# Feed-forward gate and up projections in two matmuls instead of three: the high weights times the high and low stream as one 512-wide matmul, the halves added at eviction

## The chip, the cores and the metric

The kernel runs on one core of one Trainium2 chip. The metric is the device time of one execution in microseconds, lower is better. The kernel before took 2021.01 us as the median of three runs (2017.32 to 2023.0).

## The reference, cut to what matters

Two transformer-like stacks of two layers each work on a stream of 256 tokens by 1024 channels in float32. Six feed-forward layers lie in them, and the change touches these alone. The first two (conv0, conv1) have a depthwise convolution of width 3 along the tokens between the up projection and the gate; the other four (ffn1.0, ffn2.0, ffn1.1, ffn2.1) have none.

```python
D_MODEL = 1024; SEQ = 256; D_FF = 2816
# conv0, conv1
up = depthwise_conv(h @ ffn_w_up[l], ffn_conv_w[l], ffn_conv_b[l])
f = (jax.nn.silu(up[..., :D_FF]) * up[..., D_FF:]) @ ffn_w_down[l]
h = layer_norm(DEEPNORM_ALPHA * h + f, ln_ffn_g[l], ln_ffn_b[l])
# ffn1.0, ffn2.0, ffn1.1, ffn2.1
gate, up = jnp.split(h @ wi, 2, axis=-1)      # h = rms_norm_2(x, gain)
x = x + 0.5 * ((jax.nn.silu(gate) * up) @ wo)
```

## The kernel before, in words

**Numbers.** Every float32 operand of a projection is split in two float32r parts, high and low, and a product is three matmuls in one PSUM sum: high weights times high stream, high times low, low times high (PASSES). ScalarE writes the high part of the weights as a copy with rounding (w_hi, L1302), VectorE subtracts it from the raw weights (w_lo, L1792). The stream of tokens, transposed so that channels lie on partitions, is split in the same way in xt_hi and xt_lo.

**Units.** Weights come in units of 1 MB (128 partitions x 2048 values) through a ring of three slots: SyncE loads a unit in raw, ScalarE makes w_hi, VectorE makes w_lo and counts unit_split, and TensorE uses it. A unit may be overwritten in w_hi once TensorE has begun the unit after the one that lay in its slot (unit_passed), which is two units before the new one's turn.

**Feed-forward.** The 2816 hidden channels are done in 11 chunks of 256. A chunk needs three units: gate, up, and down. TensorE's order is gate0, up0, then for each chunk c from 1 to 10 gate c, up c, down c-1, and at the end down10; chunks 1 to 10 stand in a hardware loop of five turns. A gate or up unit (up_pair, both_tiles, feature_major) is 2 tiles of 128 channels x 8 blocks k of the contraction x 3 passes = 48 matmuls of 256 columns, all in one bank of 512 values. Gate uses banks 0 and 1 in turn, up 2 and 3. A down unit is 24 matmuls of 512 columns that add to banks 4 to 7. The first gate unit is streamed: it begins when the first blocks of xt are written, k by k.

**What the other engines do with a chunk.** In the four plain layers VectorE multiplies gate's bank by the row factors rb, ScalarE takes the silu, VectorE multiplies silu with up's bank and splits the product in act_hi and act_lo (split_operand), which down needs. In the two layers with a convolution ScalarE writes the center tap of gate and of up (center, L1477), VectorE adds the two side taps of each straight from the bank (taps, four instructions of 255 columns each for gate and for up, L1789), ScalarE takes the silu, and VectorE multiplies and splits. Both engines run strictly in the order written, with the three splits of weight units of the chunk (split_in_loop) in between. On VectorE the third split stands behind split_operand.

The order of work on each engine is written out by hand; semaphores join the engines. The functions touched are both_tiles' caller up_pair and its loop in ffn_any on TensorE, chunk, center and ffn/convffn on ScalarE, gate, chunk, taps on VectorE, and one wait on GpSimd.

## Time and profile before

| | |
|---|---|
| median of three runs | 2021.01 us (2017.32 to 2023.0) |
| the profiled execution | 2020.03 us, its span 2017.5 us |
| TensorE matmul busy | 1909.7 us, 95% of the span |
| VectorE / ScalarE / GpSimd busy | 1277.4 / 893.4 / 103.2 us |
| mean granted TensorE clock | 0.949 |

The profile page gives the busy time of each engine, the busy share in 40 slices, the chain of work that ended last (who released whom, followed back from the end) and the costliest groups of instructions. Matmuls overlap in the record: one takes 283 ns from its start to its end, while the next starts after 120 ns. So durations of matmuls say little here, and starts are what is read. In the order of time a line shows its start in microseconds, its length, the engine, the source line, what is written and read, and how often it follows itself; idle time before it and what ended it stand in brackets.

### The profile page before, as it was taken

Reading aid. Unit: us, or ns where it says so; the run is one execution under the profiler, and the core shown is the slowest. Engines: PE = TensorE matmul, PEld = TensorE weight load, DVE = VectorE, ACT = ScalarE, POOL = GpSimd, SP = SyncE. Lnnn points to the kernel's source line nnn. Section 1 sums busy time; section 2 is a strip of 40 time slices with the busy share of each in tenths; the row PEclk is TensorE's granted clock in tenths of the full one; section 3 lists DMA queues with packets and bytes.
Section 4 is the critical chain, followed back from the end, with each engine's and each line's share of the span. In section 5 each row is a group of like instructions: output and inputs, shape, how many; then the busy total and the mean of one; then the engine's idle time right before and its main releaser. Section 6 shows DMA issues by size and latency. Waiting matters only on the chain.

```text
span 2017.5 us, 31210 instructions
## 1 busy us (share of the span) xinstructions
PE 1909.7 (95%) x12460; PEld 1712.2 (85%) x12460; DVE 1277.4 (63%) x1585; ACT 893.4 (44%) x1076; POOL 103.2 (5%) x79
## 2 busy tenths in 40 slices
PE   7989999988899999999988999999999989999999
PEld 7966899985699989998976888999999875789998
DVE  5787777688687776556545646556555657546555
ACT  5444444544454444335442445333533444445332
POOL 0300200030020000000060000000000000000000
PEclk9988899998899989999985999999999995999999
DMA  8531455552155545554522445555555430235553
GB/s 298 188 129 43 156 184 184 185 165 78 63 189 186 187 146 191 187 187 147 182 70 84 151 156 174 184 182 182 167 183 185 145 134 13 85 124 168 187 187 125
DMA packets 226931, 310.79 MB, mean 154 GB/s; under 512 B 6630, under 2 KB 199430, under 8 KB 226214
## 3 DMA queue, kind: packets, MB, share of 16 engines
q1 hardware_dynamic: 224038, 298.07, 44.2%
q0 software_dynamic: 2528, 10.14, 1.6%
q10 hardware_dynamic: 288, 1.52, 0.2%
q8 instruction: 53, 0.87, 0.2%
q14 instruction: 24, 0.20, 0.0%
HBM read 306.56 MB, written 3.15 MB: 154 GB/s over the span
## 4 chain that ended last, share of the span: by engine, by line
PE 85%; DVE 8%; ACT 3%; issue 2%; POOL 1%; DMA 1%; DVEq 0%; ACTq 0%
PE bank L660 43%; PE bank L887 17%; PE bank L787 8%; PE bank L683 4%; PE bank L669 3%; PE bank L960 2%; PE bank L932 2%; DVE work L1789 2%; PE bank L716 1%; ACT w_hi L1302 1%; DVE w_lo L1792 1%; PE bank L946 1%; DVE work L1792 1%; PE bank L1204 1%; DVE work L2451 1%
## 5 line engine op out<-in xcount | busy, mean ns | idle before, releaser
L1792 DVE TENSOR_TENSOR w_lo<-raw,w_hi 128x2048 fp32r<-128x2048 f32 x280 | 640.1, 2294 | 391.1 <-ACT w_hi L1302 390.7
L1302 ACT ACTIVATE w_hi<-raw 128x2048 fp32r<-128x2048 f32 x280 | 533.0, 1904 | 742.8 <-PE bank L660 467.7
L660 PE MATMUL bank<-xt_hi,w_hi 128*128 128x256 f32 x2560 | 728.4, 285 | 1.0 <-DVE w_lo L1792 1.0
L660 PE MATMUL bank<-xt_lo,w_hi 128*128 128x256 f32 x2560 | 725.5, 283 | 0.0
L660 PE MATMUL bank<-xt_hi,w_lo 128*128 128x256 f32 x2560 | 725.3, 283 | 0.0
L660 PEld LDWEIGHTS bank<-xt_hi,w_hi 128*128 128x128 f32 x2560 | 492.0, 192 | 6.5 <-issue 2.4
L660 PEld LDWEIGHTS bank<-xt_lo,w_hi 128*128 128x128 f32 x2560 | 491.9, 192 | 3.0 <-issue 0.7
L660 PEld LDWEIGHTS bank<-xt_hi,w_lo 128*128 128x128 f32 x2560 | 491.8, 192 | 0.0
L887 PE MATMUL bank<-w_hi,act_hi 128*128 128x512 f32 x528 | 206.5, 391 | 0.0
L887 PE MATMUL bank<-w_lo,act_hi 128*128 128x512 f32 x528 | 206.2, 390 | 0.0
L887 PE MATMUL bank<-w_hi,act_lo 128*128 128x512 f32 x528 | 205.4, 389 | 0.0
L887 PEld LDWEIGHTS bank<-w_hi,act_lo 128*128 128x128 f32 x528 | 99.2, 188 | 21.1
L887 PEld LDWEIGHTS bank<-w_hi,act_hi 128*128 128x128 f32 x528 | 99.4, 188 | 19.9 <-DVE act_lo L1792 0.9
L887 PEld LDWEIGHTS bank<-w_lo,act_hi 128*128 128x128 f32 x528 | 99.4, 188 | 18.2
L1789 DVE SCALAR_TENSOR_TENSOR work<-bank,par,work 128x255 f32<-128x255 f32 (+2 forms) x212 | 92.3, 478 | 23.7 <-ACT work L1477 17.3
L787 PE MATMUL bank<-w_hi,act_hi 128*128 128x512 f32 x224 | 89.9, 401 | 6.7 <-ACT work L1611 3.0
L1302 ACT ACTIVATE work<-bank 128x512 f32<-128x512 f32 (+6 forms) x88 | 46.8, 541 | 102.9 <-PE bank L946 46.5
L787 PE MATMUL bank<-w_lo,act_hi 128*128 128x512 f32 x224 | 88.9, 397 | 0.0
L787 PE MATMUL bank<-w_hi,act_lo 128*128 128x512 f32 x224 | 88.7, 396 | 0.0
L932 PE MATMUL bank<-work 128*128 128x256 f32 (+3 forms) x192 | 63.7, 505 | 18.2 <-DVE work L1792 9.1
L683 PE MATMUL bank<-xt_hi,w_hi 128*128 128x256 f32 x192 | 59.3, 309 | 18.4 <-DVE xt_lo L1789 10.7
L1477 ACT ACTIVATE work<-bank,par 128x256 f32<-128x256 f32 x88 | 44.5, 556 | 64.6 <-PE bank L660 64.6
(287 smaller groups left out, 2134.2 us busy)
## 6 DMA issues: line engine op xcount, KB each, us to landing
raw<-in_ffn_wi SPq DMA_DIRECT2D x88, 1024.0 KB, 5.1
raw<-in_ffn_w_up SPq DMA_DIRECT2D x44, 1024.0 KB, 5.1
raw<-in_ffn_wo SPq DMA_DIRECT2D x44, 1024.0 KB, 4.8
raw<-in_ffn_w_down SPq DMA_DIRECT2D x22, 1024.0 KB, 5.4
raw<-in_w_in SPq DMA_DIRECT2D x14, 1024.0 KB, 5.4
raw<-in_ssd_in_proj SPq DMA_DIRECT2D x14, 1024.0 KB, 5.3
raw<-in_mem_wkv SPq DMA_DIRECT2D x9, 1024.0 KB, 7.0
raw<-in_w_out SPq DMA_DIRECT2D x8, 1024.0 KB, 5.1
```

What stands on the lines that cost most here:

```text
L660: ins = first(mm(dst, w[s][:, k, c0:c0 + m], xt[v][:, k, :], start=k == 0 and p == 0, stop=k == KT - 1 and p == 2))
L669: ins = first(mm(dst, xt[s][:, k, P * tt:P * tt + P], w[v][:, k, c0:c0 + n], start=start and k == 0 and p == 0, stop=k == KT - 1 and p == 2))
L683: ins = first(mm(dst[:, T * j:T * j + T], w[s][:, k, P * j:P * j + P], xt[v][:, k, :], start=k == 0 and j == 0 and p == 0, stop=k == KT - ...
L716: ins = pe.transpose(bank[b][:, T * half + P * tt:T * half + P * tt + P], src[:, tt, P * k:P * k + P], ident)
L787: ins = first(mm(bank[b][:, :], act[s][:, u % 2, r, P * tt:P * tt + P], w[v][:, r, HALF * h:HALF * h + HALF], start=u == 0 and r == 0 and ...
L887: ins = first(mm(bank[b][:, :], act[s][:, c % 2, j, P * tt:P * tt + P], w[v][:, j, HALF * h:HALF * h + HALF], start=False, stop=True, skip ...
L932: ins = mm(bank[b][:, at:at + n], d["q"][t][c], d["k"][c][:, 0:n], start=c == 0, stop=c == len(d["k"]) - 1)
L960: ins = mm(bank[b][r:r + m, T * c + q0:T * c + T], v[s], prob_t[:, h % 2, T * s:T * s + T - q0], start=s == 0, stop=s == TT - 1 or d["keys ...
L1302: return act.activation(dst, src, ACT.Copy)
L1477: ins = act.activation(dst[:, c % 2, j, :], bank[b][:, T * j:T * j + T], ACT.Identity, scale=par[:, cw, at], bias=par[:, cb, at])
L1789: return dve.scalar_tensor_tensor(out=out, in0=in0, scalar=scalar, in1=in1, op0=op0, op1=op1)
L1792: return dve.tensor_tensor(out=out, in0=in0, in1=in1, op=op)
```

## The change

A gate or up unit is now 2 tiles x 8 blocks x 2 matmuls (wide_tiles). The first reads xt_hi and xt_lo of one block k as one moving operand of 512 columns (they are now two halves of one tensor, xt_both) and writes a whole bank: high times high in its columns 0 to 255, high times low in 256 to 511. The second is low weights times high stream, 256 columns, added to columns 0 to 255. A tile of 128 channels now takes a bank of its own, so gate takes banks 0 and 1 for every chunk and up 2 and 3, with no second pair to alternate with: TensorE waits for pair_drained of the last chunk before it begins the next. ScalarE copies the low halves of the two banks to f_low (low_half), and VectorE adds them to the other halves (whole); its result goes to f_gate, f_up or, in the layers with a convolution, to f_sum, from which center and taps now read. In the plain layers the multiplication of gate by rb is an instruction of its own behind the addition. In the layers with a convolution VectorE's order changes as well. The broadcast of the row factors goes through bank 4 instead of bank 1.

```diff
@@ -294,15 +302,17 @@
-        bank = [ctx.enter_context(nc.psum_tensor(f"bank{b}", [P, HALF], F32)) for b in range(8)]
+        psum = ctx.enter_context(nc.psum_tensor("bank", [P, 8, HALF], F32))
+        bank = [psum[:, b, :] for b in range(8)]
-        xt_hi = sb("xt_hi", [P, KT, T], F32R)
-        xt_lo = sb("xt_lo", [P, KT, T], F32R)
+        xt_both = sb("xt", [P, 2, KT, T], F32R)
+        xt_hi = xt_both[:, 0, :, :]
+        xt_lo = xt_both[:, 1, :, :]
...
@@ -685,6 +702,27 @@
+            def wide_tiles(b, w, first, done):
+
+                def tile(k, j):
+                    dst, part = bank[b + j], slice(P * j, P * j + P)
+                    first(mm(dst[:, :], w[0][:, k, part], xt_both[:, :, k, :], start=k == 0, stop=False,
+                             skip_group_check=True))
+                    ins = mm(dst[:, 0:T], w[1][:, k, part], xt_hi[:, k, :], start=False, stop=k == KT - 1,
+                             skip_group_check=True)
+                    if k == KT - 1 and j == 1:
+                        ins.then_inc(done, 1)
+
+                if stream_due:
+                    for k in range(KT):
+                        stream_tile(k)
+                        for j in range(2):
+                            tile(k, j)
+                else:
+                    for j in range(2):
+                        for k in range(KT):
+                            tile(k, j)
+
@@ -850,23 +888,20 @@
                     pe.wait_ge(unit_split, q0 + k + 1 if turns is None else turns * 6 + q0 + k + 1)
                     return [w[:, (q0 + k) % RING, :].rearrange("p (a b) -> p a b", a=a) for w in (w_hi, w_lo)]
-                def up_pair(k, b, turns):
-
-                    w = split_unit(k, turns, KT)
-                    both_tiles(bank[b], w, First()).then_inc(bank_full[b], 1)
-
-
-                claim(0, f"{tag}.g0")
-                up_pair(0, 0, None)
-                claim(2, f"{tag}.u0")
-                up_pair(1, 2, None)
+                def up_pair(k, i, turns):
+                    wide_tiles(2 * i, split_unit(k, turns, KT), First(), pair_full[i])
+
+                for i in range(2):
+                    for b in (2 * i, 2 * i + 1):
+                        pe.wait_ge(bank_drained[b], names.fills[b])
+                    up_pair(i, i, None)
                 if scaled:
                     pe.wait_ge(row_ready, seen.next(row_ready))
-                    claim(1, f"{tag}.rb")
+                    claim(4, f"{tag}.rb")
                     for tt in range(TT):
-                        ins = mm(bank[1][:, P * tt:P * tt + P], rcol[:, tt:tt + 1].broadcast_to([P, P]), ident,
+                        ins = mm(bank[4][:, P * tt:P * tt + P], rcol[:, tt:tt + 1].broadcast_to([P, P]), ident,
                                  start=True, stop=True)
-                    ins.then_inc(bank_full[1], 1)
+                    ins.then_inc(bank_full[4], 1)
                 for tt in range(TT):
                     for h in range(2):
                         claim(4 + 2 * tt + h, f"{tag}.{tt}{h}")
@@ -896,18 +931,15 @@
                         for tt, h in ORDER:
                             rows_of(tt, h)
-                base = {b: names.fills[b] for b in range(4)}
-                with pe.Fori(0, TURNS, 1) as i:
+                with pe.Fori(0, TURNS, 1) as turn:
                     for c in (1, 2):
                         k = 2 + 3 * (c - 1)
-                        for b, kk in ((c % 2, k), (2 + c % 2, k + 1)):
-                            pe.wait_ge(bank_drained[b], base[b] + i)
-                            up_pair(kk, b, i)
-                        down(k + 2, c - 1, i)
-                for c in (1, 2):
-                    for b, what in ((c % 2, "g"), (2 + c % 2, "u")):
-                        names.of[f"{tag}.{what}{c}"] = (b, base[b] + 1)
-                        names.fills[b] = base[b] + TURNS
+                        for i in range(2):
+                            pe.wait_ge(pair_drained[i], turn * 2 + chunk_count(tag, c - 1))
+                            up_pair(k + i, i, turn)
+                        down(k + 2, c - 1, turn)
+                for i in range(2):
+                    pe.wait_ge(pair_drained[i], chunk_count(tag, NCHUNK - 1))
                 down(len(unit_names) - 1, NCHUNK - 1, None, last=True)
                 seen.next(act_split, NCHUNK)
...
+            def low_half(tag, what, c, turn):
+                i = "gu".index(what)
+                act.wait_ge(pair_full[i], chunk_count(tag, c) if turn is None else turn * 2 + chunk_count(tag, c))
+                copy(f_low[:, 2 * i:2 * i + 2, :], psum[:, 2 * i:2 * i + 2, T:2 * T]).then_inc(low_ready, 1)
             def ffn(kind, l):
                 tag = f"{kind}.{l}"
-                def chunk(c, name, turn):
-                    b, n = names.of[name]
-                    act.wait_ge(bank_drained[b], n if turn is None else turn + n)
+                def chunk(c, turn):
+                    low_half(tag, "g", c, turn)
+                    act.wait_ge(gate_ready, seen.next(gate_ready))
                     act.activation(f_silu[:, c % 2, :], f_gate[:, c % 2, :, :], ACT.Silu).then_inc(silu_ready, 1)
+                    low_half(tag, "u", c, turn)
...
+                def center(c, what, dst, tile0, turn):
+                    low_half(tag, what, c, turn)
+                    i = "gu".index(what)
+                    act.wait_ge(pair_drained[i], chunk_count(tag, c) if turn is None else turn * 2 + chunk_count(tag, c))
+                    for j in range(2):
+                        t = tile0 + 2 * c + j
+                        at = bass.ds(44 + t, 1) if turn is None else bass.ds(turn * 4 + 44 + t, 1)
+                        ins = act.activation(dst[:, c % 2, j, :], f_sum[:, 2 * i + j, :], ACT.Identity,
+                                             scale=par[:, cw, at], bias=par[:, cb, at])
+                    ins.then_inc(center_ready, 1)
+                def chunk(c, turn):
+                    center(c, "g", f_gate, 0, turn)
+                    center(c, "u", f_up, 22, turn)
+                    if turn is not None:
+                        split_in_loop(tag, 3 * c + 3, turn)
+                    act.wait_ge(taps_ready, seen.next(taps_ready))
+                    act.activation(f_silu[:, c % 2, :], f_gate[:, c % 2, :, :], ACT.Silu).then_inc(silu_ready, 1)
...
@@ -2040,24 +2081,27 @@
                 if split_next[0] < len(split_order):
                     split_late.append(True)
+            def whole(tag, what, c, turn, dst):
+                i = "gu".index(what)
+                dve.wait_ge(low_ready, seen.next(low_ready))
+                dve.wait_ge(pair_full[i], chunk_count(tag, c) if turn is None else turn * 2 + chunk_count(tag, c))
+                tt_(dst, psum[:, 2 * i:2 * i + 2, 0:T], f_low[:, 2 * i:2 * i + 2, :],
+                    ALU.add).then_inc(pair_drained[i], 1)
+                dve.wait_ge(pair_drained[i], chunk_count(tag, c) if turn is None else turn * 2 + chunk_count(tag, c))
             def ffn(kind, l):
                 tag = f"{kind}.{l}"
                 def gate(c, turn):
-                    b, n = names.of[f"{tag}.g{c}"]
-                    dve.wait_ge(bank_full[b], n if turn is None else turn + n)
-                    tt_(f_gate[:, c % 2, :, :], two(bank[b][:, :]), spread(rb[:, :], 2),
-                        ALU.mult).then_inc(bank_drained[b], 1)
+                    whole(tag, "g", c, turn, f_gate[:, c % 2, :, :])
+                    tt_(f_gate[:, c % 2, :, :], f_gate[:, c % 2, :, :], spread(rb[:, :], 2),
+                        ALU.mult).then_inc(gate_ready, 1)
                 def chunk(c, turn):
+                    whole(tag, "u", c, turn, f_up[:, c % 2, :, :])
                     dve.wait_ge(silu_ready, seen.next(silu_ready))
-                    b, n = names.of[f"{tag}.u{c}"]
-                    dve.wait_ge(bank_full[b], n if turn is None else turn + n)
-                    tt_(f_raw[:, c % 2, :], f_silu[:, c % 2, :], bank[b][:, :],
-                        ALU.mult).then_inc(bank_drained[b], 1)
-                    dve.wait_ge(bank_drained[b], n if turn is None else turn + n)
+                    step(tt_(two(f_raw[:, c % 2, :]), two(f_silu[:, c % 2, :]), f_up[:, c % 2, :, :], ALU.mult))
                     split_operand(c % 2, two(f_raw[:, c % 2, :]))
                 split()
...
+                def total(c, what, turn):
+                    i = "gu".index(what)
+                    whole(tag, what, c, turn, f_sum[:, 2 * i:2 * i + 2, :])
+                def taps(c, what, dst, tile0, turn):
                     dve.wait_ge(center_ready, seen.next(center_ready))
-                    b, n = names.of[name]
+                    i = "gu".index(what)
                     for g, side in ((wa, 0), (wb, 1)):
                         for j in range(2):
                             t = tile0 + 2 * c + j
                             w = par[:, g, bass.ds(t, 1) if turn is None else bass.ds(turn * 4 + t, 1)]
                             part = dst[:, c % 2, j, 1:T] if side == 0 else dst[:, c % 2, j, 0:T - 1]
-                            src = bank[b][:, T * j:T * j + T - 1] if side == 0 else bank[b][:, T * j + 1:T * j + T]
+                            src = f_sum[:, 2 * i + j, 0:T - 1] if side == 0 else f_sum[:, 2 * i + j, 1:T]
                             ins = stt(part, src, w, part, ALU.mult, ALU.add)
                         if side == 0:
                             step(ins)
-                    ins.then_inc(bank_drained[b], 1)
+                    return ins
                 def chunk(c, turn):
-                    taps(c, f"{tag}.g{c}", f_gate, 0, turn)
-                    taps(c, f"{tag}.u{c}", f_up, 22, turn)
-                    b, n = names.of[f"{tag}.u{c}"]
-                    dve.wait_ge(bank_drained[b], n if turn is None else turn + n)
+                    total(c, "g", turn)
+                    if turn is not None:
+                        split_in_loop(tag, 3 * c + 2, turn)
+                    taps(c, "g", f_gate, 0, turn).then_inc(taps_ready, 1)
+                    total(c, "u", turn)
+                    if turn is not None:
+                        split_in_loop(tag, 3 * c + 3, turn)
+                    step(taps(c, "u", f_up, 22, turn))
                     dve.wait_ge(silu_ready, seen.next(silu_ready))
                     step(tt_(two(f_raw[:, c % 2, :]), two(f_silu[:, c % 2, :]), f_up[:, c % 2, :, :], ALU.mult))
                     split_operand(c % 2, two(f_raw[:, c % 2, :]))
-                    if turn is not None:
-                        split_in_loop(tag, 3 * c + 3, turn)
```

Where the instructions now stand is shown at two places. The first is VectorE in the loop of the two layers with a convolution, the second (up) half of a chunk. Before, from the wait for the center tap to the splits of the next units:

```order
L1789 ISA [waits center_ready]
L1789 SCALAR_TENSOR_TENSOR work<-bank,par,work 128x255
...
L1789 ISA [waits vec_step]
L1789 SCALAR_TENSOR_TENSOR work<-bank,par,work 128x255
...
L1792 TENSOR_TENSOR work<-work 128x512 [waits silu_ready]
L1827 CAST act_hi<-work 128x512 [waits vec_step]
L1792 TENSOR_TENSOR act_lo<-work,act_hi 128x512 [waits vec_step]
L1792 TENSOR_TENSOR w_lo<-raw,w_hi 128x2048 [waits hi_ready]
```

Now the same place, in which low_ready is ScalarE's copy of the low halves, pair_full_u TensorE's end of the up unit, and hi_ready ScalarE's split of the unit after next:

```order
L1833 TENSOR_TENSOR work<-bank,work 128x512 [waits pair_full_u,low_ready]
L1862 REGISTER_ALU [waits pair_drained_u]
L1833 TENSOR_TENSOR w_lo<-raw,w_hi 128x2048 [waits hi_ready]
L1830 ISA [waits center_ready]
L1830 SCALAR_TENSOR_TENSOR work<-work,par 128x255
...
L1830 ISA [waits vec_step]
L1830 SCALAR_TENSOR_TENSOR work<-work,par 128x255
...
L1833 TENSOR_TENSOR work<-work 128x512 [waits silu_ready,vec_step]
L1868 CAST act_hi<-work 128x512 [waits vec_step]
L1833 TENSOR_TENSOR act_lo<-work,act_hi 128x512 [waits vec_step]
```

The addition is new, and the split of the third unit moved from behind the last subtraction to ahead of the up taps.

The second place is TensorE at the start of a plain layer, from the end of up0 to the first matmul of gate1. Before:

```order
L867 MATMUL bank1<-con,rcol 128x128 [waits bank_drained1,row_ready]
L867 MATMUL bank1<-con,rcol 128x128
L874 MATMUL bank4<-zero 128x512 [waits bank_drained4]
L874 MATMUL bank5<-zero 128x512 [waits bank_drained5]
...
L850 ISA [waits bank_drained1]
L660 MATMUL bank1<-xt_hi,w_hi 128x256 [waits unit_split]
```

Now:

```order
L902 MATMUL bank<-con,rcol 128x128 [waits bank_drained4,row_ready]
L902 MATMUL bank<-con,rcol 128x128
L909 MATMUL bank<-zero 128x512 [waits bank_drained4]
L909 MATMUL bank<-zero 128x512 [waits bank_drained5]
...
L888 ISA [waits pair_drained_g]
L709 MATMUL bank<-xt,w_hi 128x512 [waits unit_split]
L711 MATMUL bank<-xt,w_lo 128x256
```

The four zeroing matmuls now stand behind the drain of the row factors' bank, and gate1 behind VectorE's addition of gate0 instead of behind that drain alone.

## Rows read from the trace of the kernel before

**Rows 1.** The page, parts 1 and 4.

```profile
PE 1909.7 (95%) x12460; PEld 1712.2 (85%) x12460; DVE 1277.4 (63%) x1585; ACT 893.4 (44%) x1076; POOL 103.2 (5%) x79
PE bank L660 43%; PE bank L887 17%; PE bank L787 8%; PE bank L683 4%; PE bank L669 3%; PE bank L960 2%; PE bank L932 2%; DVE work L1789 2%; PE bank L716 1%; ACT w_hi L1302 1%; DVE w_lo L1792 1%; PE bank L946 1%; DVE work L1792 1%; PE bank L1204 1%; DVE work L2451 1%
```

**Rows 2.** Chain in order of time in conv0: start us, length us, what.

```profile
297.92 11.51 PE bank L660 x96
...
394.33 5.47 PE bank L887 x24
399.81 3.03 PE bank L887 x12
```

**Rows 3.** TensorE in order of time: 27 matmuls in a row, then 14.

```profile
624.74 0.28 PE L660 MATMUL bank<-xt_hi,w_hi 128*128 128x256 f32 x1
...
627.86 0.28 PE L660 MATMUL bank<-xt_hi,w_lo 128*128 128x256 f32 x1
...
1282.64 0.39 PE L887 MATMUL bank<-w_lo,act_hi 128*128 128x512 f32 x1
...
1285.59 0.39 PE L887 MATMUL bank<-w_hi,act_lo 128*128 128x512 f32 x1
```

**Rows 4.** VectorE in order of time, one chunk of conv0.

```profile
305.78 2.29 DVE L1792 TENSOR_TENSOR w_lo<-raw,w_hi 128x2048 fp32r<-128x2048 f32 x1 [3.46 <-ACT w_hi L1302]
307.99 1.89 DVE L1789 SCALAR_TENSOR_TENSOR work<-bank,par,work 128x255 f32<-128x255 f32 x4
...
312.98 0.69 DVE L1792 TENSOR_TENSOR work<-work 128x512 f32<-128x512 f32 x1 [0.32 <-ACT work L1489]
313.71 0.43 DVE L1827 CAST act_hi<-work 128x512 fp32r<-128x512 f32 x1
...
314.77 4.52 DVE L1792 TENSOR_TENSOR w_lo<-raw,w_hi 128x2048 fp32r<-128x2048 f32 x2
```

**Rows 5.** ScalarE in order of time, the same chunk.

```profile
309.61 1.02 ACT L1477 ACTIVATE work<-bank,par 128x256 f32<-128x256 f32 x2 [2.95 <-PE bank L660]
310.52 1.91 ACT L1302 ACTIVATE w_hi<-raw 128x2048 fp32r<-128x2048 f32 x1
```

**Rows 6.** Groups by line and shape: count, busy us, mean ns, idle before.

```profile
L1789 DVE SCALAR_TENSOR_TENSOR work<-work,par 128x256 f32<-128x256 f32 x134 | 56.6, 479 | 0.8 <-DVE work L1789 0.4
L1792 DVE TENSOR_TENSOR work<-work,bank 128x512 f32<-128x512 f32 x46 | 31.7, 689 | 63.0 <-PE bank L660 56.8 <-ACT work L1452 4.5 <-PE bank L1093 1.8
L1302 ACT ACTIVATE work<-bank 128x512 f32<-128x512 f32 x51 | 29.9, 592 | 57.2 <-PE bank L946 29.2 <-POOL mix L2604 16.8 <-PE bank L660 6.7
```

**Rows 7.** Start of ffn1.1: ScalarE's drain of rb; the chain on TensorE.

```profile
1425.92 0.38 ACT L1302 ACTIVATE rb<-bank 128x256 f32<-128x256 f32 x1 [4.10 <-PE bank L867]
...
1425.89 0.96 PE bank L874 x4
1426.85 11.71 PE bank L660 x96
```

**Rows 8.** Start of ffn1.0: VectorE's splits; the chain.

```profile
764.83 4.49 DVE L1792 TENSOR_TENSOR w_lo<-raw,w_hi 128x2048 fp32r<-128x2048 f32 x2 [1.50 <-ACT w_hi L1302]
...
767.18 11.77 PE bank L660 x96
```

**Rows 9.** VectorE ahead of gate0 of ffn1.1.

```profile
1412.11 2.68 DVE L1789 SCALAR_TENSOR_TENSOR xt_lo<-bank,par,xt_hi 128x256 fp32r<-128x256 f32 x6 [0.58 <-ACT xt_hi L1335]
```

**Rows 10.** TensorE after idle time; a stretch, with granted clock behind POOL's busy time.

```profile
408.86 1.94 PE L716 MATMUL bank<-con,mix 128*128 128x128 f32 x16 [3.31 <-DVE mix L1979]
...
746.34 3.65 PE L716 MATMUL bank<-con,mix 128*128 128x128 f32 x16 [3.31 <-DVE mix L1979]
...
751.30:755.20 3.90, 3.89 (x18) 3.90 (x19) 3.80 (x7) 1.41 (x4) 0.00 (x0) 0.50 0.00 0
```

**Rows 11.** VectorE and GpSimd near the start of conv0.

```profile
232.86 2.53 DVE L1827 CAST act_hi<-work 128x512 fp32r<-128x512 f32 x1
...
232.35 2.75 POOL L2524 TENSOR_TENSOR x<-x,wide 128x1024 f32<-128x1024 f32 x1
```

More of the change, by code:

```diff
@@ L202, in weight_units, with chunk_count @@
     return place
+FFN_ORDER = ("conv0", "conv1", "ffn1.0", "ffn2.0", "ffn1.1", "ffn2.1")
+def chunk_count(tag, c):
+    return NCHUNK * FFN_ORDER.index(tag) + c + 1
 class Count:
@@ L2615, in swa @@
             def swa():
-                full("ffn1.1.g0")
+                pool.wait_ge(pair_full[0], chunk_count("ffn1.1", 0))
                 pool.dma_start(w_bias[0:1, 0:D], inp["attn_bo_2"][0:1, :]).then_inc(small_in, 16)
```

32 lines of the change are left out of this document (17 added, 15 removed).

## The prediction

> **What bounds the kernel now.** I read the page first [rows 1]: TensorE's matmuls fill 95% of the span, and in the chain that ended last the gate and up line L660 alone holds 43%, the down line L887 17%. The reader is to see that VectorE, at 63%, isn't the bound on average. Then the chain in order of time [rows 2]: inside a feed-forward layer it holds nothing but TensorE, 96 matmuls of a gate and an up unit in 11.51 us and 24 of a down unit in 5.47 us, so a chunk takes 16.98 us, and what is saved on TensorE is saved for good as long as nobody else is late. Third, TensorE's starts [rows 3]: 26 steps of 256 columns take 3.12 us, or 0.1200 us each; 13 steps of 512 columns take 2.95 us, or 0.2269 us each. Two narrow ones cost 0.2400, one wide one 0.2269. The columns are the same, so a matmul with its weight load has a fixed part of about 13 ns.
>
> **The gain.** There are 6 layers x 11 chunks x 2 units x 2 tiles x 8 blocks = 2112 places where two narrow matmuls become one wide. 2112 x 0.0131 = 27.7 us. At the half clock there is no fixed part to save: 18 matmuls of 256 columns in 3.90 us are 0.217 each [rows 10], which is 256 columns at 1.2 GHz. The cold start of gate0 in ffn1.0, and the same taken for conv0, take 0.3 off: 27.4 us. A chunk should take 16.98 - 32 x 0.0131 = 16.56 us.
>
> The row says 13 ns. The Trainium skill (TensorE: Matmul & The Clock Gate, "Wait — 56ns, not 53.3ns?") has start-to-start of a warm matmul at N / 2.4 GHz plus about 2.5 ns. By that the gain would be 2112 x 2.5 ns = 5.3 us, an estimate from that page. The trace disagrees with it and decides; the sum doesn't use it.
>
> No matmul before reads its moving operand in two runs. I bound its extra cost by 0 from below (the down matmul reads 512 in one run at 0.2269) and by 13 ns from above, at which a wide one costs as much as two narrow ones. I take 0, since the column rate is the same in both rows of starts. The Trainium skill (SBUF — State Buffer, "Door 1: The DMA port swizzle (why `[64,N]` ≈ `[32,N]`)", the note on cachelines) says that accesses that stay on a 16-byte line run at full bandwidth; the two runs here are 1 KB each, so by it too nothing is lost. No run before shows it.
>
> **What is added.** Per chunk ScalarE gets two copies of 128x512 out of PSUM, near 0.59 us each, and VectorE two additions of 128x512 with one operand in PSUM, near 0.69 us each [rows 6]. In the plain layers gate's addition is new beside the multiplication, and so is up's. The side taps now read both operands from SBUF: 479 ns there [rows 6] against four in 1.89 us with one from PSUM [rows 4], no difference. In the plain layers VectorE has three splits at 2.29 and some 4 us of small work in 16.56 us; the copies and additions hide behind up and down.
>
> **Layers with a convolution, in the loop.** VectorE's round per chunk, from starts [rows 4, 5]: three splits x 2.22 (305.78 to 307.99) = 6.7; taps 2 x 1.9 = 3.8; product, cast and subtraction 312.98 to 314.77, 1.8; additions 2 x 0.72 = 1.4. Then a wait that is new: the third split now stands between up's addition and up's taps, ScalarE splits its part behind the center tap, and the center tap waits for that addition. ScalarE's center pair to its split is 0.91 (309.61 to 310.52), the split 1.91, with hand-overs 2.9 in all. Sum 16.6, beside TensorE's 16.56. So the two engines are level. I take no stall per chunk in the loop, with a bound of 0.6 us per chunk above (below). Without that wait in the order VectorE had 13.7 us of work and the cover would be ample.
>
> **Layers with a convolution, at the end.** Down10 follows down9 without another gate and up between. It needs act_lo of chunk 10, and before that came just in time: down9 starts at 394.33 and takes 5.47, and down10 starts at 399.81, with no idle time [rows 2]. Now, from the end of gate10 (t): ScalarE first splits the unit after (to t+2.0, released by the start of up10), copies the low half (t+2.6), VectorE adds (3.3), splits (5.5), taps (7.4), adds up (8.1), ScalarE does center and split (11.0), VectorE splits (13.2), taps (15.1), product, cast, subtraction and hand-over (17.1). TensorE is ready at t + 5.55 (up10) + 5.47 (down9) = 11.0. Stall 6.0 us, twice: 12.1. TensorE idle for 3.31 us was followed by transposes at half speed, 16 in 3.65 us [rows 10], and by matmuls at granted clock 0.50, 1.2 GHz, in the 3.9 us from 751.30. After 6 us of idle I expect the same: some 3.4 us of down10 at half rate, 1.7 us lost, twice: 3.4. Bounds 0 and 2 each.
>
> **Plain layers, at the start.** ffn2.0, ffn1.1, ffn2.1: before, gate1 starts at 1426.85 behind the zeroing matmuls, which ran from 1425.89 beside the drain of rb (1425.92 to 1426.30) [rows 7]. Now the zeroing waits for that drain (0.45 later), and gate1 waits for ScalarE's copy (0.59) and VectorE's addition (0.69) behind the drain, so it starts near 1427.7: 0.9 later, three times: 2.7. In ffn1.0 VectorE is late at this point: its two splits run from 764.83 to 769.3, and gate1 starts at 767.18, behind the first [rows 8]. The addition of gate0 stands behind both, so gate1 starts at 770.1: 2.9 later, and 0.3 of gain in gate0 and up0 is lost with it. I add 0.5 for a chance that the clock falls in that gap: 3.7.
>
> **Streamed gate0.** It now waits for banks 0 and 1, that is for block 3 of xt instead of block 2. In the plain layers with a stream from PSUM blocks come every 0.45 us (six in 2.68) [rows 9], and TensorE needs 0.7 per block, so it can't catch up: 3 x 0.45 = 1.3. In conv0, conv1 and ffn1.0 ScalarE has drained both banks by then: 0.
>
> **Sum.** Against the profiled execution, 2020.03 us (span 2017.5 and 2.5 around it): -27.4 + 12.1 + 3.4 + 2.7 + 3.7 + 1.3 = -4.2 us. Beside them GpSimd: near 232 us its additions of 2.75 us go along with a cast of 2.53 us on VectorE that takes 0.43 elsewhere [rows 11, 4]. VectorE's round in conv0 and conv1 now has more reads from SBUF and no slack at its start; 0.5 each: -3.2. The profiled execution is 1.0 below the median of the runs; from one or the other I get 2016.8 to 2017.8. I say 2017.
>
> **The rivals.**
> A. VectorE's side costs less: the clock doesn't fall in the gaps, and the end stall is nearer 5 us since hand-overs overlap. For it: the transposes at 408.86, also after 3.31 us of idle, took 1.94 us for 16, near full speed [rows 10]. Against: 6 us of idle is almost twice 3.31. Sum: -3.2 - 3.4 - 2 = -8.6: 2011.
> B. Slower: the loops of conv0 and conv1 become bound by VectorE. The round is 16.6 by durations; six more waits per chunk on VectorE at 0.1 us each make 17.2, and from 16.56 on each tenth counts in 20 rounds: 0.6 x 20 = 12, so 2029. For it: no slack is left, and a new ring ScalarE to VectorE to ScalarE to VectorE lies in each round. Against: the waits that exist cost 0.03 us, as between product and cast (312.98 + 0.69 to 313.71) [rows 4].
> C. The change doesn't do what it says: the wide matmul costs as much as two narrow ones, by its two-run operand or since the fixed part belongs to bytes and not to instructions. The gain vanishes and the costs stay: 2044. Against: the starts [rows 3]. By the page's 2.5 ns (TensorE: Matmul & The Clock Gate, in the Trainium skill) it would come out near here too, at 2039, an estimate.
>
> **How the numbers follow.** Forecast (gain and costs nearly cancel, 2013 to 2021) 0.55, A (2008 to 2013) 0.22, B (2023 to 2032) 0.16, C 0.04, others 0.03. What a measurement of this kernel can tell from no change is about 0.3%, 6 us: below 2015.0 is faster, above 2027.1 slower. Faster takes all of A and a fourth of the forecast: 0.35. Slower is most of B and C: 0.15. Same is the rest, 0.50. The range leaves out C and the tails of A and B: 2008 to 2027.
>
> **What the profile after would show.** Right: starts of a wide and a narrow one 0.347 us apart; 16.56 us per chunk in ffn loops; TensorE waiting for VectorE's act_lo at the end of conv0 and conv1 for 6 us, with the clock at 0.5 behind it; gate1 waiting in the plain layers 0.9 us, in ffn1.0 some 4 us in all. Wrong: a pair above 0.36 us (C), chunks of conv0 above 16.7 us with TensorE waiting for w_lo or act_lo in the loop (B), or no wait at the ends (A).

## The result and the profile after

The changed kernel takes 2048.42 us (median of 4 runs, 2044.95 to 2053.49), the kernel before on the same chip 2019.16 (4 runs). The ratio is 1.014, with a 95% interval of 1.0119 to 1.0161. It is slower by 29 us where I forecast some 3 less; the time lies outside my range (2008 to 2027), and "slower" had 0.15. A kernel's time is always the median over its executions in the fast state; the only other one, of 10147.63 us in experiment 8, is left out.

The page of the changed kernel, parts 1 and 4, against [rows 1]:

```profile
PE 1910.4 (93%) x10348; PEld 1607.5 (79%) x10348; DVE 1360.9 (67%) x1717; ACT 966.3 (47%) x1208; POOL 102.7 (5%) x79
PE 80%; DVE 10%; ACT 4%; issue 4%; POOL 1%; DMA 1%; DVEq 0%; ACTq 0%
```

TensorE has 2112 instructions less and is as long busy: what the pairs save is made up by stretches at half clock, in which a matmul is longer (down10, gate1 of ffn1.0 and others below), so the busy time hides the gain. VectorE and ScalarE now hold 14% of the chain that ended last. Starts of the same work in both chains show where:

| from there | before, us | after, us | after minus before |
|---|---|---|---|
| output rows of mixer 0 | 185.00 | 184.73 | -0.3 |
| down10 of conv0 | 399.81 | 408.86 | +9.1 |
| output rows of mixer 1 | 524.72 | 535.51 | +10.8 |
| down10 of conv1 | 737.30 | 760.43 | +23.1 |
| last downs of ffn1.0 | 931.77 | 959.64 | +27.9 |
| output rows ahead of ffn2.0 | 1196.23 | 1226.78 | +30.6 |
| last downs of ffn1.1 | 1591.38 | 1621.73 | +30.4 |
| last downs of ffn2.1 | 2003.34 | 2031.67 | +28.3 |

The two convolution layers and ffn1.0 lose nearly all of it. Of the other plain layers ffn2.0 loses 0.5 us, ffn1.1 and ffn2.1 gain 0.7 and 1.2. Of the step of 2.7 between ffn1.0 and the rows ahead of ffn2.0, 1.5 us are taken up below.

**The loop.** Down units of ffn2.1 in the chain (start, length):

```profile
1981.29 5.50 PE bank L922 x24
1998.08 5.50 PE bank L922 x24
2014.87 5.50 PE bank L922 x24
```

A chunk takes 16.79 us, not 16.56 ([rows 2]: 16.98 before). Its pairs, and those of up0 in the same layer (a start to the next start of L709 is a pair):

```profile
1887.62 0.40 PE L709 MATMUL bank<-xt,w_hi 128*128 128x512 f32 x1
...
1889.04 0.40 PE L709 MATMUL bank<-xt,w_hi 128*128 128x512 f32 x1
```

```profile
1861.93 0.39 PE L709 MATMUL bank<-xt,w_hi 128*128 128x512 f32 x1
...
1862.96 0.40 PE L709 MATMUL bank<-xt,w_hi 128*128 128x512 f32 x1
```

Four pairs in 1.42, three in 1.03. Over a whole unit it is 5.30 us for 15 pairs in the loops (0.3533 each), and 5.20 in up0 (0.3467, the value that I forecast from [rows 3]). The 0.3533 lies between that and the 0.36 that I had set as the sign of rival C.

**The end of conv0.** VectorE, then ScalarE, then TensorE in order of time:

```profile
391.78 2.29 DVE L1833 TENSOR_TENSOR w_lo<-raw,w_hi 128x2048 fp32r<-128x2048 f32 x1
393.98 0.68 DVE L1833 TENSOR_TENSOR work<-bank,work 128x512 f32<-128x512 f32 x1
394.79 2.29 DVE L1833 TENSOR_TENSOR w_lo<-raw,w_hi 128x2048 fp32r<-128x2048 f32 x1
...
398.82 0.68 DVE L1833 TENSOR_TENSOR work<-bank,work 128x512 f32<-128x512 f32 x1
402.59 2.29 DVE L1833 TENSOR_TENSOR w_lo<-raw,w_hi 128x2048 fp32r<-128x2048 f32 x1 [3.09 <-ACT w_hi L1334]
```

```profile
399.67 1.09 ACT L1518 ACTIVATE work<-work,par 128x256 f32<-128x256 f32 x2 [3.25 <-DVE work L1833]
400.67 1.89 ACT L1334 ACTIVATE w_hi<-raw 128x2048 fp32r<-128x2048 f32 x1
```

```profile
408.86 0.77 PE L922 MATMUL bank<-w_hi,act_hi 128*128 128x512 f32 x1 [8.73 <-DVE act_lo L1833]
409.43 0.63 PE L922 MATMUL bank<-w_lo,act_hi 128*128 128x512 f32 x1
...
412.84 0.63 PE L922 MATMUL bank<-w_hi,act_hi 128*128 128x512 f32 x1
```

The ring that I named is there: up's addition (398.82), ScalarE's center tap and split, VectorE's split 3.09 us later. TensorE waits 8.73 us here and 9.0 in conv1. Then matmuls stand 0.43 apart instead of 0.2267, which is 512 columns at 1.2 GHz (512 / 1.2 GHz = 0.427 us), until about 413.3; in the stretch from 408.90 to 413.00 the granted clock is 0.50, 1.2 GHz. Down10's first twelve take 5.23 us against 3.03 [rows 2].

**The start of conv0.** VectorE's taps for the first gate, with GpSimd beside them:

```profile
229.10 6.14 DVE L1830 SCALAR_TENSOR_TENSOR work<-work,par 128x255 f32<-128x255 f32 x4 [1.24 <-ACT work L1518]
```

```profile
229.57 2.46 POOL L2573 TENSOR_TENSOR x<-mix,wide 128x1024 f32<-128x1024 f32 x1
232.11 2.45 POOL L2574 TENSOR_TENSOR x<-x,wide 128x1024 f32<-128x1024 f32 x1
```

Four taps take 6.14 us, and end after GpSimd has. In the loop they take 1.90. Down0 starts 1.9 us later behind gate0's start than before in conv0, 3.9 in conv1; some 1.6 of the 3.9 are one unit (from 586.67) that runs in part at half clock, 7.10 us from its first to its last start instead of 5.53.

**The start of ffn1.0.** Who TensorE waited for from 776 to 977 us (total, times, longest):

```profile
PE bank L909 <- ACT rb L1334: 3.0, 1, 3.0
PE bank L709 <- DVE work L1833: 2.0, 1, 2.0
PE bank L902 <- DVE rcol L2074: 0.5, 1, 0.5
```

5.5 us where one wait of 1.0 stood before [rows 8], and gate1 behind it runs cold: 15 pairs in 7.33 us instead of 5.30. What ends last is not the wait for rb but VectorE, its two splits and then the addition of gate0:

```profile
789.81 4.49 DVE L1833 TENSOR_TENSOR w_lo<-raw,w_hi 128x2048 fp32r<-128x2048 f32 x2 [1.50 <-ACT w_hi L1334]
794.22 0.68 DVE L1833 TENSOR_TENSOR work<-bank,work 128x512 f32<-128x512 f32 x1
```

```profile
795.03 0.79 PE L709 MATMUL bank<-xt,w_hi 128*128 128x512 f32 x1 [2.00 <-DVE work L1833]
```

VectorE's two splits start 24.98 us later than before (764.83 in [rows 8]), just as gate0 does, and gate1 starts 27.85 later (767.18 there): the start of the layer costs 2.9 us. The waits grew by more, 4.5, because TensorE came to them earlier: gate0 takes 5.63 us at full clock, and took 7.59 before (751.31 to 758.90), when it began at half clock ([rows 10], the stretch from 751.30).

In ffn2.0, ffn1.1 and ffn2.1 the waits for rb and for gate0's sum are 0.5 and 0.3.

### The profile page after: what moved, and what is told of

It is laid out like the page before. It is cut to its first block, busy times and chain, and to the rows that moved or that the text cites. A ratio compares the mean times of both kernels' runs of the same rounds, so it can differ in the third digit from the quotient of the medians.

```text
span 2045.8 us, 27424 instructions
## 1 busy us (share of the span) xinstructions
PE 1910.4 (93%) x10348; PEld 1607.5 (79%) x10348; DVE 1360.9 (67%) x1717; ACT 966.3 (47%) x1208; POOL 102.7 (5%) x79
## 4 chain that ended last, share of the span: by engine, by line
PE 80%; DVE 10%; ACT 4%; issue 4%; POOL 1%; DMA 1%; DVEq 0%; ACTq 0%
PE bank L709 23%; PE bank L922 17%; PE bank L711 11%; PE bank L825 7%; PE bank L677 5%; PE bank L686 3%; DVE work L1830 2%; PE bank L992 2%; PE bank L700 2%; PE bank L964 2%; ACT w_hi L1334 2%; DVE w_lo L1833 1%; DVE work L1833 1%; PE bank L754 1%; PE bank L978 1%
## 5 line engine op out<-in xcount | busy, mean ns | idle before, releaser
L709 PE MATMUL bank<-xt,w_hi 128*128 128x512 f32 x2112 | 755.0, 401 | 16.5 <-DVE work L1833 6.5
L711 PE MATMUL bank<-xt,w_lo 128*128 128x256 f32 x2112 | 595.4, 282 | 0.0
L709 PEld LDWEIGHTS bank<-xt,w_hi 128*128 128x128 f32 x2112 | 400.2, 189 | 119.9 <-issue 6.5
L711 PEld LDWEIGHTS bank<-xt,w_lo 128*128 128x128 f32 x2112 | 402.1, 190 | 2.1
L677 PE MATMUL bank<-xt,w_hi 128*128 128x256 f32 (+1 forms) x1088 | 200.6, 287 | 0.0
L1334 ACT ACTIVATE work<-bank 128x512 f32<-128x512 f32 (+5 forms) x220 | 124.1, 568 | 135.3 <-PE bank L978 46.8
L677 PEld LDWEIGHTS bank<-xt,w_hi 128*128 128x128 f32 (+1 forms) x1088 | 171.1, 193 | 1.6 <-issue 1.4
L1830 DVE SCALAR_TENSOR_TENSOR work<-work,par 128x255 f32<-128x255 f32 (+3 forms) x319 | 148.1, 513 | 12.7 <-ACT work L1518 5.0
L677 PE MATMUL bank<-xt,w_lo 128*128 128x256 f32 (+1 forms) x544 | 154.7, 284 | 0.0
L677 PEld LDWEIGHTS bank<-xt,w_lo 128*128 128x128 f32 (+1 forms) x544 | 104.8, 193 | 0.0
```

The lines of the kernel that those rows point to most:

```text
L677: ins = first(mm(dst, w[s][:, k, c0:c0 + m], xt[v][:, k, :], start=k == 0 and p == 0, stop=k == KT - 1 and p == 2))
L709: first(mm(dst[:, :], w[0][:, k, part], xt_both[:, :, k, :], start=k == 0, stop=False, skip_group_check=True))
L711: ins = mm(dst[:, 0:T], w[1][:, k, part], xt_hi[:, k, :], start=False, stop=k == KT - 1, skip_group_check=True)
L1334: return act.activation(dst, src, ACT.Copy)
L1830: return dve.scalar_tensor_tensor(out=out, in0=in0, scalar=scalar, in1=in1, op0=op0, op1=op1)
```

## The experiments

All are edits of the changed kernel. The kernel before, timed beside each of them, took 2020.4 to 2021.8 us. Under each text on record stands what came out.

**1. The layout of the stream.**

```diff
-        xt_both = sb("xt", [P, 2, KT, T], F32R)
+        xt_both = sb("xt", [P, KT, 2, T], F32R)
```

> The changed kernel, with the high and low stream of one block side by side ([P, KT, 2, T]), so that the wide matmul reads one run of 512 values instead of two of 256; nothing else moves. In the changed kernel a wide and a narrow matmul take 0.3533 us in the loops (15 spacings in 5.30) but 0.3467 in up0 of ffn2.0 (5.20). Theory 1: the two runs of the moving operand cost these 6.4 ns. Then pairs stand at 0.347 everywhere, a chunk takes 16.6 instead of 16.79, and the kernel comes 2112 x 0.0064 = 13 us below the changed one: 2035. Rival: the spacing has another cause (the same code runs at both values); pairs stay at 0.353, time within 2 us of 2048.

2053.2 us, and the plain chunk is still 16.79:

```profile
1984.79 5.50 PE bank L922 x24
2001.59 5.50 PE bank L922 x24
```

The two runs of the operand cost nothing. Theory 1 fell. The time is 4.8 us above the changed kernel's, which neither text expected; in the profiled execution 5.1 us more than there lie between down10 of conv0 and down0 of conv1, so mixer 1 and the start of conv1, and the chunks are the same.

**2. VectorE's third split moved back.**

```diff
 total(c, "u", turn)
-if turn is not None:
-    split_in_loop(tag, 3 * c + 3, turn)
 ...
 split_operand(c % 2, two(f_raw[:, c % 2, :]))
+if turn is not None:
+    split_in_loop(tag, 3 * c + 3, turn)
```

> The changed kernel with VectorE's third split of a chunk back behind the split of the product, in the two layers with a convolution. Theory 2 (the moved split makes the end stall): gate's and up's last steps no longer wait for ScalarE's split (1.9) and VectorE's (2.29) between up's addition and up's taps. The wait of down10 for act_lo falls from 8.7 us to 4.5 or less in each of the two layers, and the cold first 12 matmuls (5.23 us against 3.03) shorten too: 8 to 17 us less, 2031 to 2040. Rival: VectorE's round is full (three splits, taps and additions fill 16.8 us), so it is late in whatever order; the wait stays above 7 and the time near 2047.

2042.4 us. The two waits for act_lo fall from 8.7 and 9.0 to 3.0 each:

```profile
PE bank L922 <- DVE act_lo L1833: 6.0, 2, 3.0
```

So 5.7 and 6.0 us of them came from the moved split. Down10's first twelve still take 4.28 and 4.51: the clock can fall after 3 us of idle, and it need not. In experiment 11 conv1's down10 waits 3.41 us and then runs at full clock:

```profile
754.90 0.47 PE L928 MATMUL bank<-w_hi,act_hi 128*128 128x512 f32 x1 [3.41 <-DVE act_lo L1841]
```

```profile
754.90 3.02 PE bank L928 x12
```

At the starts of conv0 and conv1 waits were added (4.5 and 4.7 us ahead of L709), so 6 us of some 13 arrived.

**3. The sum left in PSUM** (convolution layers): VectorE's addition writes the bank, center and taps read it, and the last tap drains it.

> The changed kernel, with the sum of the halves in the convolution layers left in PSUM: VectorE adds in place, center and side taps read the bank, and the bank is drained by the taps. Theory 3: four side taps took 6.14 us at 229.10 because both their operands lie in SBUF while GpSimd adds; before, with one operand in PSUM, four took 1.79 beside the same additions (229.93). Then they take 1.8 here, and the waits at the start of conv0 and conv1 (1.9 and 3.9 us later down0 than before) go: 4 to 5 us less, 2043 to 2044. Rival: GpSimd's traffic slows VectorE whatever it reads, or the later drain of the banks makes TensorE wait: 2048 or more. The end stall should stay near 8.7 by both.

2049.6 us: the taps became fast as expected, and the gain didn't come. The taps beside the same additions of GpSimd:

```profile
229.30 1.78 DVE L1831 SCALAR_TENSOR_TENSOR work<-bank,par,work 128x255 f32<-128x255 f32 x4 [1.17 <-ACT work L1519]
```

```profile
229.83 2.37 POOL L2580 TENSOR_TENSOR x<-mix,wide 128x1024 f32<-128x1024 f32 x1
```

1.78 us against 6.14, with one operand in PSUM instead of none. The Trainium skill (SBUF — State Buffer, "Who interferes with whom") says that a VectorE instruction with two inputs in SBUF contends with a GpSimd instruction that reads SBUF, and one with at most one such input doesn't; both traces agree. Behind gate0's start down0 comes 0.7 us earlier than in the changed kernel in conv0 and 2.9 later in conv1, where TensorE waits 3.8 us for VectorE's taps, which now free the banks. There ScalarE's split of the third unit also comes late (VectorE waits 2.72 us for it, 0.62 in the changed kernel). So these runs do not show that the slow taps alone made the starts late. And from the fourth chunk on the banks are drained late, and a conv0 chunk takes 16.97 to 17.16 us: the rival's second half.

**4. The change in the plain layers alone.**

> The changed form in the four plain layers alone; conv0 and conv1 are as they were before the change. By the stages of the two profiles conv0 takes 12.3 us and conv1 some 13.5 more than before, and the four plain layers together with what lies between them some 3 more. If these stages are independent, this kernel takes 2048.4 - 26 = 2022, 3 above before. Rival 1: the plain layers gain once they aren't entered late or cold; 2010 to 2015. Rival 2: the wide form slows the rest of the program by more than its own stages (2030 and above).

2022.9 us, as the stages say: the two convolution layers cost 25.5 us. The plain layers cost 2 or nothing, since the ratio to the kernel before is 1.0016 (0.9996 to 1.0036).

**5. Groups of eight.**

```diff
-        for k in range(KT):
-            tile(k, j)
+        for k in range(KT):
+            wide(k, j)
+        for k in range(KT):
+            narrow(k, j)
```

> The changed kernel, where a tile's eight wide matmuls now stand ahead of its eight narrow ones instead of in turns (gate0 of a layer stays in turns, since its blocks arrive one by one). All spacings are multiples of 3.33 ns: 0.120 is 36 of them, 0.2267 is 68, the pair in loops 106 where 36 + 68 = 104. Theory 4: each change between the widths costs one such step. With two changes per tile instead of sixteen a tile takes 8 x 0.3467 = 2.77 us and not 2.83, a chunk 16.6, and the kernel comes 12 us below the changed one: 2036. Rival: the 106 come from something else in the state of the engine (power, other engines' traffic); a tile stays at 2.83 and the time within 2 us of 2048.

2044.6 us. A plain chunk takes 16.61:

```profile
1977.60 5.47 PE bank L928 x24
1994.21 5.47 PE bank L928 x24
```

That is the 0.18 per chunk that was expected, and it came in the plain layers alone, where the loops are 6.3 us shorter in all. 3.8 us of the expected 12 arrived: gate0 of ffn1.1 and of ffn2.1 ran 1.5 and 1.6 us longer than in the changed kernel. In conv0 the chunk stays at 16.76, though TensorE could be faster. There the chain that ends last runs through VectorE, whose splits for the down units come every 16.76 us and hold the first matmuls of the down unit up by some 0.15:

```profile
308.29 2.28 DVE w_lo L1839
325.05 2.29 DVE w_lo L1839
```

**6. Edits 2 and 3 together.**

> Both edits of the last two experiments on the convolution layers: VectorE's third split back behind the product's split, and the sum of the halves left in PSUM. With the split moved alone the kernel took 2042.4, down10 waited 3.0 us in each layer, and the first up and gate units of a layer waited for VectorE 4.5 us in three times, which the side taps of 6.1 us beside GpSimd explain. Theory 3: with taps of 1.8 us these waits at the start go, so 2 x 4 us less: 2034 to 2036. Rival: the taps now free the banks late (in the in-place form TensorE waited 0.15 to 0.3 us before up units in the loop), which takes the gain back: 2041 to 2044.

2037.4 us, 5.0 less than edit 2 alone, between the 2034 to 2036 of theory 3 and the rival's 2041. The loop is back at 16.79, so the later drain does no harm once the third split is out of the way. One wait at the start of each layer remains (3.4).

**7. TensorE kept busy in the gap.**

```diff
+if not scaled:
+    for _ in range(34):
+        mm(bank[0][:, :], xt_hi[:, 0, 0:P], xt_both[:, :, 0, :], start=True, stop=True, ...)
 down(len(unit_names) - 1, NCHUNK - 1, None, last=True)
```

> The changed kernel with 34 matmuls of 512 columns between down9 and down10 in conv0 and conv1, which write a bank that nobody reads any more: 7.7 us of work in a gap of 8.7 us. It is extra work, nothing is left out. Theory 5 (idle TensorE lowers its clock): down10's first 12 matmuls take 2.8 us instead of 5.23, at granted clock 1.0, and the wait for act_lo shrinks to about 1 us behind the added ones; 2 x 2.4 = 5 us less than the changed kernel: 2043 to 2044. Rival: the 5.23 us come from late operands (act_lo and the last split arrive piece by piece), not from the clock; 2048.

2041.2 us, 7.3 less. The first matmul of down10 in order of time, and the chain's first twelve:

```profile
408.84 0.50 PE L922 MATMUL bank<-w_hi,act_hi 128*128 128x512 f32 x1 [0.79 <-DVE act_lo L1837]
```

```profile
408.84 3.03 PE bank L922 x12
```

The operand comes at the same moment (408.84 against 408.86), and the twelve take 3.03 us instead of 5.23. So the slow matmuls were the clock, and not late operands. The profiled executions differ by 4.4 us (2043.2 against 2047.6), which is what the two down10 give; nothing more comes behind them. The other 2.9 us between the medians lie within what each kernel's own executions differ by (2038.9 to 2044.4 and 2045.0 to 2053.5).

**8. Plain layers alone, groups of eight, gate0's copy and addition ahead of the second split.**

> The changed form in the plain layers alone (2022.9 in that form), with the widths grouped as in the experiment above, and at the start of a plain layer ScalarE's copy of gate0's low half and VectorE's addition ahead of the second split. By theory 4 a plain layer gains 10 chunks x 0.19 = 1.9 us, four of them 8; the earlier addition takes away TensorE's wait ahead of gate1 in ffn1.0 (2.0 + 3.0 us for VectorE's work and for rb, of which 1 was there before) and some of 0.3 to 0.5 in the others: 3 more. 2011 to 2013. If grouping changes nothing: 2019 to 2020. If the early addition pushes the second split behind TensorE's need of it: 2 us above either.

2014.1 us, the median of the seven executions that count, ratio to before 0.9966 (0.9948 to 0.9984). Theory 4's 2011 to 2013 is just missed. With the eighth the median is 2016.0, the figure that the texts of experiments 9 and 11 use.

**9. The same, groups of sixteen, row factors ahead of the second split.**

```diff
-for j in range(2):
-    for k in range(KT):
-        wide(k, j)
-    for k in range(KT):
-        narrow(k, j)
+for part in (wide, narrow):
+    for j in range(2):
+        for k in range(KT):
+            part(k, j)
```

> The best version so far (wide form in the plain layers alone, early addition of gate0, 2016.0) with all sixteen wide matmuls of a unit ahead of its sixteen narrow ones, and ScalarE's copy of the row factors ahead of its second split. With groups of eight a plain chunk took 16.61 us, and of the eight wide ones behind narrow ones about five stood at 0.233 and the rest at 0.227. Theory 4a (a wide matmul runs at 0.233 for some matmuls behind narrow ones): one such stretch per unit instead of two, 2 x 5 x 0.0067 = 0.07 per chunk less at most, 16.54 to 16.58; four layers 1 to 3 us; with the earlier row factors 2013 to 2015. Rival: no further gain, 16.61 and 2016.

2007.6 us, ratio 0.9935 (0.9919 to 0.9950): faster than both kernels. Chunks take 16.57 to 16.58, 16.565 being 32 x 0.3467 + 5.47:

```profile
1959.46 5.47 PE bank L938 x24
1976.03 5.47 PE bank L938 x24
```

In ffn1.0 the waits for rb and for gate0's sum are now these:

```profile
PE bank L709 <- DVE work L1862: 1.3, 1, 1.3
PE bank L925 <- ACT rb L1362: 0.6, 1, 0.6
```

1.9 us instead of 5.0 in the changed kernel (2.4 in experiment 8). The time is lower than I expected, 2013 to 2015, and not by merit of the edit alone. The profiled executions of 8 and 9 differ by 8.3 us. Of these 1.4 are the chunks. 3.0 lie ahead of down0 of conv0, where the two kernels are the same and the granted clock (third number from the right) was 0.78 and 0.86:

```profile
100.00:184.00 84.00, 75.41 (x366) 51.55 (x364) 66.26 (x125) 35.07 (x71) 2.52 (x2) 0.78 0.24 81
100.00:184.00 84.00, 74.37 (x386) 51.65 (x384) 69.50 (x132) 38.61 (x77) 2.52 (x2) 0.86 0.26 82
```

And 3.2 lie in gate0 of ffn1.1 and ffn2.1, 7.2 us each in 8 and 5.6 in 9. Whether the edit made these two run warm the runs don't tell. Against the kernel before, the gain holds over six executions.

**10. Two wide, two narrow, block by block** (changed kernel: wide to bank 0, wide to bank 1, narrow to 0, narrow to 1).

> The changed kernel with the two tiles of a unit interleaved block by block: wide to bank 0, wide to bank 1, narrow to bank 0, narrow to bank 1. Rival theory B1 (a narrow matmul waits since it adds to the bank that the wide one just before it still writes): no two in a row share a bank now, so four matmuls take 0.693 (two pairs of 0.3467), a plain chunk 16.57 and the kernel 2040 or less. Theory 4a (what counts is that wide ones stand behind narrow ones, with some five matmuls until they are back at 0.227): both wide ones of a block stand within five of a narrow one, so the pair stays at 0.353, the chunk at 16.79 and the kernel at 2048.

2044.1 us, the plain chunk 16.59:

```profile
1991.55 5.45 PE bank L927 x24
2008.13 5.45 PE bank L927 x24
```

Theory 4a fell, and theory 4 with it, by which half as many changes of the width would make 16.68. The bank remained.

**11. All mends in all layers.**

> Wide form in all six layers with every mend that helped: groups of sixteen, VectorE's third split behind the product's, sum of the convolution layers left in PSUM, early addition of gate0, row factors ahead of the second split. The form with the two convolution mends alone took 2037.4. The plain layers should give 7 to 9 us as they did between 2022.9 and 2016.0. In the convolution loops, with groups of eight, the chunk stayed at 16.76 with no wait of TensorE longer than its record shows while plain chunks took 16.61: VectorE's round (three splits, additions, taps, and 3.1 us of waiting for ScalarE's split) is the bound there. If so they stay at 16.76, and the kernel takes 2028 to 2031, over the version that leaves the convolution layers alone. Rival: with the new order VectorE is no longer the bound, chunks fall to 16.57 there too, and the kernel reaches 2024 or less.

2022.6 us, ratio 1.0007 (0.9995 to 1.0018). Plain chunks take 16.57, those of conv0 16.70 to 16.77, mean 16.73, with the same matmuls. Once per chunk the first two wide matmuls of the up unit come 0.16 us late, when VectorE's split for that unit ends; VectorE itself is idle for 2.9 us per chunk, most of it behind ScalarE's copies and center taps. So VectorE's side bounds the chunk, by the waits between the two engines and not by work alone. The time is the one that the rival named, but not for its reason, since these chunks did not fall to 16.57. It is still 15 us above version 9, which differs in the convolution layers alone.

**12. Turns, but each narrow one in the other bank.**

> The changed kernel with wide and narrow matmuls in turns as in it, but each narrow one adds to the other bank than the wide one just before it (wide to bank 0, the narrow of the block before to bank 1, wide to bank 1, narrow to bank 0). It tells two explanations of the 0.3533 us pair apart. B1 (a narrow matmul directly behind a wide one in the same bank waits): the pair takes 0.347 and the plain chunk 16.57 to 16.6. Theory 4b (every change of the width costs one or two steps of 3.33 ns, whatever the bank): as many changes as in the changed kernel, so the pair stays at 0.353 and the plain chunk at 16.79. The time follows the plain layers alone, since VectorE's round holds the convolution loops at 16.76: 2042 to 2044 by B1, 2048 by 4b.

2046.1 us. The chunk is 16.75:

```profile
1995.79 5.46 PE bank L930 x24
2012.53 5.46 PE bank L930 x24
```

The bank isn't it either. Strict turns of wide and narrow cost 0.353 per pair in nearly all units of the loops, pairs of each 0.348, groups of sixteen 0.3467. Why stays open, and so does why some units in turns run at 0.3467. In the changed kernel up0 of every layer but ffn1.1 does, and gate1 and up1 of ffn2.1 too. That last up1 takes 5.43 us from its first to its last start, and 5.54 in experiment 6, where its code is the same. So the order of the widths alone does not fix the spacing.

## Why the prediction was wrong, step by step

The forecast was -3.2 us against before; the spans of the profiled executions differ by +28.3. The terms:

- **The gain, -27.4.** The step that failed is the addition of a wide and a narrow spacing, each of which I had from a run of its own kind [rows 3]: 0.2269 + 0.1200. In turns they take 0.3533. A chunk gained 0.19 instead of 0.42, over 60 chunks 14 us; 4 of these would have been lost in the 20 convolution chunks in any case, by the next term. I bounded the wide matmul for its two-run operand, which costs nothing (experiment 1), and not for its neighbour. Rival C had the direction, but half the gain stayed.
- **The round of VectorE in the convolution loops, 16.6.** It is 16.76 (experiment 5), 16.73 at best (11). So rival B was right that VectorE takes the lead there, at 0.17 to 0.20 per chunk and not 0.6, and the slower pairs covered it: in the changed kernel the later chunks of conv0 take 16.79 and TensorE waits for nobody in them.
- **The end of the convolution layers, +12.1.** It was 17.7. The mechanism stood as written (experiment 2). The walk left out the down unit's split: ScalarE's copy of gate's low half is there at 391.65, VectorE begins that split at 391.78 and adds only at 393.98. That is 2.3 us per layer, nearly all of what is missing.
- **Cold clock, +3.4.** It was 4.4, all in down10 (2 x (5.23 - 3.03), experiment 7). Rival A, that the clock doesn't fall, was wrong here: it fell after 8.7 and 9.0 us of idle, and in experiment 2 after 3.0. It could hold after such short waits, as [rows 10] had left open: it did after 3.41 us in experiment 11.
- **The starts of the convolution layers, +1.0.** They were 1.9 + 3.9. "Both operands from SBUF, no difference" rested on a tap without GpSimd beside it [rows 6]. [Rows 11] showed VectorE slowed beside GpSimd on a cast; before, the taps were spared by their operand in PSUM (experiment 3). That the slow taps are what made the starts late is argued and only in part shown: with fast taps conv0 started 0.7 us earlier and conv1 didn't (experiment 3), and part of conv1's 3.9 is clock.
- **ffn1.0, +3.7.** It was 4.9: gate1 started 2.9 later, by the walk that I had written, and then ran cold for 2.0, where I had put 0.5. The zeroing behind ScalarE's two splits and rb (3.0) was not in the walk and cost nothing, since VectorE's addition came later still. I had also counted gate0's cold start as it was before; it ran warm, and that gained nothing either, since gate1 waited for VectorE.
- **The other plain layers, +4.0.** Gate1 waits 0.8 and gate0 1.9 instead of 1.4 or 1.5: as forecast. What no term held is that gate0 of ffn2.0 takes 7.19 us instead of 5.85, at granted clock 0.50 from 1253.40 to 1256.80: 1.3 us. It took 7.2 in every experiment too, and what makes it cold isn't shown.
- **Chance.** The 192 matmuls after ffn1.0 took 24.81 us here, with the granted clock at 0.58 from 976.80 to 981.00, and 23.27 before. With ffn1.0 in the wide form they took 23.26 or 23.27 in experiments 1, 4, 5 and 6 and 24.9 to 25.2 in 2, 3 and 7: 1.5 us that the change doesn't make.

The shortfalls, 14 + 5.6 + 1.0 + 4.8 + 1.2 (ffn1.0's) + 1.3 (gate0 of ffn2.0) + 1.5, are 29.4, against 31.5 between -3.2 and +28.3. Of the 2.1 that are missing, 0.9 are late chunks in the convolution loops (nine chunks in 151.31 and 151.82 us, where 9 x 16.79 is 151.1); the rest isn't located. The ends were moved by experiment 2 and the clock in down10 by 7; the pair's loss was removed in the plain layers by 5 and 9 with its cause open; the starts stay in part argued.

What failed in the judgement: I gave three independent costs their likeliest value each, at places where the engine behind has no slack, and a range that held one of them going wrong.

## What to carry to other kernels

Spacings measured in runs of one matmul size need not add up when the sizes take turns: measure the sequence, and where two sizes must mix, try them in groups. A sum of waits is not what a stage costs: in ffn1.0 they grew by 4.5 us and the start by 2.9. A form that shifts work to VectorE pays where VectorE has slack for a whole round and for the chain at the last chunk (plain layers, with experiment 9's order: 13 us faster), and not where its round equals TensorE's; decide it layer by layer. Before an operand moves from PSUM to SBUF, look at what GpSimd does at that moment.

## What was not expected of the hardware

- Four taps of 128x255 with both operands in SBUF: 6.14 us beside GpSimd's additions, 1.90 without them; with one operand in PSUM 1.78 beside the same additions.
- A 512-wide and a 256-wide matmul in strict turns: 0.3533 us per pair in the loops, 0.3467 when grouped by sixteen, and at times in turns too. Neither the layout of the moving operand nor the bank made a difference (experiments 1, 12).
- After 3.0 us of idle TensorE fell to the half clock within the next matmuls (4.28 and 4.51 us for twelve instead of 3.03, experiment 2), and after 3.41 us it once did not (3.02, experiment 11). With filler in the gap and 0.8 us of idle left it stayed up (3.03, experiment 7).
